# Attention of a two-layer diffusion block: exponentials turned by transposes, division at the values' eviction, outputs turned back per pair, and the next queries computed three units early

## The reference, cut to what matters

```
def attend(q, k, v):
    s = jnp.einsum('bqhd,bkhd->bhqk', q, k).astype(jnp.float32) * SOFTMAX_SCALE
    p = jax.nn.softmax(s, axis=-1).astype(v.dtype)
    return jnp.einsum('bhqk,bkhd->bqhd', p, v)
```

## Time and profile before

| | |
|---|---|
| median of three runs | 2633.77 us |
| profiled execution: its time, its span | 2636.96 us, 2635.1 us |
| busy: PE, DVE, ACT | 2461.8 us (93%), 1775.2 us (67%), 1396.1 us (53%) |
| chain that ended last | PE 86%, DVE 8%, ACT 3%, issue 1%, DMA 1% |
| attention, layer 0: first scores to first `gv` matmul | 160.03 to 291.56 us |
| attention, layer 1: the same | 1158.65 to 1234.29 us |

### The profile page before, as it was taken

How to read it: one execution, slowest core, us unless ns; L and a number is a source line. 1 busy time by engine, 2 the same in 40 slices (tenths; PEclk the granted TensorE clock), 3 DMA queues, 4 the chain that set the end, 5 groups by cost and what they waited for, 6 DMA issues and landing times.

```text
span 2635.1 us, 32564 instructions
## 1 busy us (share of the span) xinstructions
PE 2461.8 (93%) x12206; PEld 1980.5 (75%) x12206; DVE 1775.2 (67%) x1876; ACT 1396.1 (53%) x1495; POOL 42.5 (2%) x84
## 2 busy tenths in 40 slices
PE   6989999998999997878798599999999999999997
PEld 3756768884787885657697588888888888888886
DVE  3556863435333334667664788888989898989886
ACT  3354453334222222454554576777777777777775
POOL 0001000001000000000000000000000000000000
PEclk8988989999999998988898799999999999999998
DMA  7234223344434334211362798989999999999894
GB/s 270 78 120 136 80 64 104 112 162 167 143 110 130 117 94 145 80 64 47 96 202 75 287 371 341 377 341 356 361 353 354 354 370 343 371 356 362 340 374 183
DMA packets 104683, 579.23 MB, mean 220 GB/s; under 512 B 11920, under 2 KB 13840, under 8 KB 54800
## 3 DMA queue, kind: packets, MB, share of 16 engines
q1 hardware_dynamic: 93072, 536.04, 55.4%
q0 software_dynamic: 11520, 41.95, 4.7%
HBM read 576.89 MB, written 1.05 MB: 219 GB/s over the span
## 4 chain that ended last, share of the span: by engine, by line
PE 86%; DVE 8%; ACT 3%; issue 1%; DMA 1%; SPq 0%; DVEq 0%; ACTq 0%
PE bank L560 24%; PE bank L561 24%; PE bank L562 24%; PE bank L719 2%; PE bank L741 2%; PE bank L623 2%; PE bank L729 2%; DVE cacc L1453 1%; PE bank L913 1%; DVE rstd L1394 1%; PE bank L975 1%; PE bank L598 1%; DVE t L1409 1%; DVE al L1415 1%; DVE wlo L1374 1%
## 5 line engine op out<-in xcount | busy, mean ns | idle before, releaser
L1738 DVE TENSOR_TENSOR elo<-eraw,ehi 128x2048 fp32r<-128x2048 f32 x388 | 885.1, 2289 | 144.8 <-ACT ehi L1299 143.7
L1299 ACT CAST ehi<-eraw 128x2048 fp32r<-128x2048 f32 x388 | 742.4, 1916 | 263.1 <-PE bank L562 257.3
L1374 DVE TENSOR_TENSOR wlo<-raw,whi 128x1024 fp32r<-128x1024 f32 x220 | 269.5, 1225 | 298.6 <-ACT whi L1023 296.9
L560 PE MATMUL bank<-ah,whi 128*128 128x512 f32 (+1 forms) x1088 | 401.1, 369 | 23.4 <-DVE al L1415 15.6
L560 PE MATMUL bank<-ehi,xgh 128*128 128x512 f32 x1024 | 406.2, 397 | 17.9 <-DVE xgl L1744 17.9
L561 PE MATMUL bank<-elo,xgh 128*128 128x512 f32 x1024 | 400.1, 391 | 0.0
L562 PE MATMUL bank<-ehi,xgl 128*128 128x512 f32 x1024 | 399.6, 390 | 0.0
L561 PE MATMUL bank<-al,whi 128*128 128x512 f32 (+1 forms) x1088 | 392.1, 360 | 0.0
L562 PE MATMUL bank<-ah,wlo 128*128 128x512 f32 (+1 forms) x1088 | 391.9, 360 | 0.0
L1023 ACT CAST whi<-raw 128x1024 fp32r<-128x1024 f32 x220 | 229.6, 1044 | 119.1 <-PE bank L562 119.0
L560 PEld LDWEIGHTS bank<-ah,whi 128*128 128x128 f32 x1088 | 209.2, 192 | 70.6 <-DVE al L1415 17.5
(11 more groups left out here) (266 smaller groups left out, 2865.2 us busy)
## 6 DMA issues: line engine op xcount, KB each, us to landing
eraw<-in_moe SPq DMA_DIRECT2D x388, 1024.0 KB, 4.8
raw<-in_dense SPq DMA_DIRECT2D x220, 512.0 KB, 3.6
mod_b<-in_mod POOLq DMA_DIRECT2D x48, 512.0 KB, 4.9
mod_a<-in_mod POOLq DMA_DIRECT2D x32, 512.0 KB, 3.9
mod_s<-in_mod SPq DMA_DIRECT2D x16, 512.0 KB, 12.9
hres<-in_xT SPq DMA_DIRECT2D x1, 2048.0 KB, 8.3
wsT<-in_wsT SPq DMA_DIRECT2D x2, 512.0 KB, 8.5
out_h<-hres SPq DMA_DIRECT2D x2, 512.0 KB, 2.9
```

The source lines that it names most:

```text
L560: pe.matmul(dst, wh, xh, start=first, stop=False, skip_group_check=True)
L1299: nc.scalar.copy(ehi[c % ESPLIT][:], eraw[c % ERAW][:]).then_inc(e_hi, 1)
L1374: dve.tensor_tensor(wlo[c % SPLIT][:], raw[c % RAW][:], whi[c % SPLIT][:].bitcast(F32), ALU.subtract).then_inc(w_lo, 1)
L1738: dve.tensor_tensor(elo[c % ESPLIT][:], eraw[c % ERAW][:], ehi[c % ESPLIT][:].bitcast(F32), ALU.subtract).then_inc(e_lo, 1)
```

## The change

`turn` becomes plain transposes of the exponentials and waits for the exponential itself; `diag` and its ACT instruction go. `values` has the operands swapped: the turned exponentials are stationary (128x128), 64 columns of `V` move, and the output is 128 queries x 64 features. ACT divides when it evicts it, into a new tile `otok`. When all units of a pair are in `otok`, PE transposes it into an `acc_bank` (new step `outputs`), ACT copies that to `oh` and DVE subtracts for `ol`, one instruction each to a pair. Queries of pair j+1 are made in the step three before its first unit, into a second tile `qT2` that lies where `wsT` is; so `wsT` and `bsp` are loaded after the last scores, by SP, which waits for them. The end of the loop is one step later.

```
@@ plan: order of products
         for j in range(4):
             chunks.append(("uq", L, j))
             accs += [("uq", L, j, h) for h in range(2)]
+            if j > L:
+                accs.append(("ot", L, j - 1 - L))
+        accs += [("ot", L, j) for j in range(3 - L, 4)]
@@ tiles
-        rinv = place("rinv", [P, 2], F32)
+        rinv = place("rinv", [P, 4], F32)
-        diag = place("diag", [P, 2, P], F32, w1 + 36864)
+        qT2 = place("qT2", [QK_HEAD, 2, TOK], F32, wsT_at)
+        otok = place("otok", [P, 4, P], F32, std_at)
@@ new helpers
+        def pair_units(L):
+            return len(UNITS[L]) // 4
+        def query_pair(L, s):
+            j, r = divmod(s + 3, pair_units(L))
+            if s == 0:
+                return 0
+            return j if r == 0 and 1 <= j < 4 else None
+        def output_pair(L, s):
+            j, r = divmod(s - 3, pair_units(L))
+            return j - 1 if r == 0 and 1 <= j <= 4 else None
@@ SP
-                    if c == CHUNK[("q0", L)]:
-                        if L:
-                            sp.wait_ge(sp_done, 4 * L)
+                    if c == CHUNK[("gv", L, 2)]:
+                        sp.wait_ge(sc_ready, sum(len(UNITS[i]) for i in range(L + 1)))
                         sp.dma_start(wsT[:], A["wsT"][L]).then_inc(layer_landed, 16)
                         sp.dma_start(bsp[:], A["bsp"][L]).then_inc(layer_landed, 16)
@@ PE (queries(j): the 18 matmuls, moved out of scores unchanged)
                 def turn(u):
                     lo, hi = keys_of(units[u][2])
-                    pe.wait_ge(p_ready, base_u + u + 1)
+                    pe.wait_ge(exp_ready, base_u + u + 1)
                     if base_u + u:
                         pe.wait_ge(pt_ready, base_u + u)
                     for i in range((hi - lo) // P):
-                        mm = pe.matmul(TB[:, i * P:(i + 1) * P], pr[:, u % 2, i * P:(i + 1) * P], diag[:, u % 2, :],
-                                       start=True, stop=True, skip_group_check=True)
+                        mm = pe.transpose(TB[:, i * P:(i + 1) * P], pr[:, u % 2, i * P:(i + 1) * P], ident[:])
...
-                        mm = pe.matmul(o_bank[u % 2][64 * h:64 * h + 64, 0:P],
+                        mm = pe.matmul(o_bank[u % 2][:, 0:VH], pT[:, u % 2, i * P:(i + 1) * P],
                                        V[:, lo // P + i, (2 * j + h) * VH:(2 * j + h + 1) * VH],
-                                       pT[:, u % 2, i * P:(i + 1) * P], start=(i == 0), stop=(i == nk - 1))
+                                       start=(i == 0), stop=(i == nk - 1))
+                def outputs(j):
+                    pe.wait_ge(o_ready, base_u + (j + 1) * pair_units(L))
+                    b = bank(("ot", L, j))
+                    for t in range(nq // P):
+                        mm = pe.transpose(b[:, t * P:(t + 1) * P], otok[:, t, :], ident[:])
+                    mm.then_inc(ot_psum, 1)
...
-                for s in range(len(units) + 3):
+                for s in range(len(units) + 4):
+                    if s == 0:
+                        queries(0)
                     if s < len(units):
                         scores(s)
                     if 2 <= s <= len(units) + 1:
                         turn(s - 2)
-                    if s >= 3:
+                    if output_pair(L, s) is not None:
+                        outputs(output_pair(L, s))
+                    if 3 <= s <= len(units) + 2:
                         values(s - 3)
+                    if s and query_pair(L, s) is not None:
+                        queries(query_pair(L, s))
@@ ACT, step s: copies of the queries last; no diag; then
+                    out_j = output_pair(L, s)
+                    if out_j is not None:
+                        act.wait_ge(ot_psum, 4 * L + out_j + 1)
+                    if 3 <= s <= len(units) + 2:
                         u = s - 3
                         j, h, t = units[u]
+                        act.wait_ge(rinv_ready, base_u + u + 1)
                         act.wait_ge(o_psum, base_u + u + 1)
-                        nc.scalar.copy(oh[64 * h:64 * h + 64, j, t * P:(t + 1) * P],
-                                       o_bank[u % 2][64 * h:64 * h + 64, 0:P]).then_inc(x_hi, 1)
+                        nc.scalar.activation(otok[:, t, 64 * h:64 * h + 64], o_bank[u % 2][:, 0:VH], ACT.Copy,
+                                             scale=rinv[:, u % 4:u % 4 + 1]).then_inc(o_ready, 1)
+                    if out_j is not None:
+                        b = acc_bank[ACC[("ot", L, out_j)] % 2]
+                        nc.scalar.copy(oh[:, out_j, 0:nq], b[:, 0:nq]).then_inc(x_hi, 1)
+                    if s and query_pair(L, s) is not None:
+                        take_queries(query_pair(L, s))
@@ DVE, step s: row maximum and its negative first, then
+                    if 1 <= s <= len(units):
+                        u = s - 1
+                        dve.wait_ge(exp_ready, base_u + u + 1)
+                        if base_u + u >= 4:
+                            dve.wait_ge(o_ready, base_u + u - 3)
+                        dve.reciprocal(rinv[:, u % 4:u % 4 + 1], rsum[:, u % 2:u % 2 + 1]).then_inc(rinv_ready, 1)
+                    taps(TAPS_UNIT[L])
+                    out_j = output_pair(L, s)
+                    if out_j is not None:
                         dve.wait_ge(x_hi, n.next(x_hi))
+                        a = ACC[("ot", L, out_j)]
+                        dve.tensor_tensor(ol[:, out_j, 0:nq], acc_bank[a % 2][:, 0:nq],
+                                          oh[:, out_j, 0:nq].bitcast(F32), ALU.subtract).then_inc(acc_free[a % 2], 1)
+                    if s and query_pair(L, s) is not None:
+                        turn_queries(query_pair(L, s))
```

More of the change, by code:

```diff
@@ L393, in build @@
         o_ready = sem("o_ready")
+        ot_psum = sem("ot_psum")
         vt_ready = sem("vt_ready")
@@ L700, in _, with queries @@
                 units = UNITS[L]
+                def queries(j):
+                    wh, wl = weights(("uq", L, j))
+                    for hh_ in range(2):
+                        b = bank(("uq", L, j, hh_))
+                        for k in range(3):
+                            cols = slice((k * 2 + hh_) * P, (k * 2 + hh_ + 1) * P)
+                            mm = mm3(b[:, 0:nq], wh[:, cols], wl[:, cols], cnh[:, 2 + k, 0:nq],
+                                     cnl[:, 2 + k, 0:nq], k == 0, k == 2)
+                        mm.then_inc(chunk_used if hh_ else part, 1)
                 def scores(u):
@@ L704, in scores @@
                     if (h, t) == (0, 0):
-                        wh, wl = weights(("uq", L, j))
-                        for hh_ in range(2):
-                            b = bank(("uq", L, j, hh_))
-                            for k in range(3):
-                                cols = slice((k * 2 + hh_) * P, (k * 2 + hh_ + 1) * P)
-                                mm = mm3(b[:, 0:nq], wh[:, cols], wl[:, cols], cnh[:, 2 + k, 0:nq],
-                                         cnl[:, 2 + k, 0:nq], k == 0, k == 2)
-                            mm.then_inc(chunk_used if hh_ else part, 1)
                         taken(pe, ("uv", L, 3))
+                        taken(pe, ("uq", L, j, 0))
                         taken(pe, ("uq", L, j, 1))
@@ L1141, in _, with take_queries @@
                     act.wait_ge(const_landed, 16 * n_const)
-                for s in range(len(units) + 3):
-                    if L == 0 and s >= KD and s % KD == 0:
-                        copy_rows(1 + s // KD)
-                    if s < len(units):
-                        j, h, t = units[s]
-                        if (h, t) == (0, 0):
-                            for hh_ in range(2):
-                                key = ("uq", L, j, hh_)
-                                b, free = (await_acc if hh_ else await_part)(key, ("uq", L, j))
-                                if nq == TOK:
-                                    nc.scalar.copy(qT[64:96, hh_, LAT:TOK], b[64:96, LAT:TOK])
-                                nc.scalar.copy(qT[0:64, hh_, 0:nq], b[0:64, 0:nq]).then_inc(sig_ready, 1)
+                def take_queries(j):
+                    for hh_ in range(2):
+                        key = ("uq", L, j, hh_)
+                        b, free = (await_acc if hh_ else await_part)(key, ("uq", L, j))
+                        if nq == TOK:
+                            nc.scalar.copy(qT_of(j)[64:96, hh_, LAT:TOK], b[64:96, LAT:TOK])
+                        nc.scalar.copy(qT_of(j)[0:64, hh_, 0:nq], b[0:64, 0:nq]).then_inc(sig_ready, 1)
+                for s in range(len(units) + 4):
+                    if L == 0 and s >= KD and s % KD == 0 and s <= len(units):
+                        copy_rows(1 + s // KD)
+                    if s == 0:
+                        take_queries(0)
                     if 2 <= s <= len(units) + 1:
@@ L1161, in _ @@
```

(7 more changed lines are left out.)

51 lines of the change are left out of this document (18 added, 33 removed).

## The result

The changed kernel takes 2575.53 us (median of four runs, 2572.96 to 2579.59) against 2634.16 us for the kernel before on the same chip: ratio 0.9778, 95% interval 0.9758 to 0.9798. The prediction said 2579 us with a range of 2566 to 2603. Its profiled execution has a span of 2573.6 us where the one before had 2635.1, so 61.5 us have to be accounted for.

| stretch | before | after | difference |
|---|---|---|---|
| start to layer 0's first scores | 160.03 | 157.09 | -2.9 |
| layer 0, first scores to first `gv` matmul | 131.53 | 95.45 | -36.1 |
| from there to layer 1's first scores | 867.1 | 865.4 | -1.7 |
| layer 1, first scores to first `gv` matmul | 75.64 | 53.04 | -22.6 |
| from there to the end | 1400.8 | 1402.6 | +1.8 |

The account below looks back on a forecast made before the run. PE, 86% of the span, was taken as the bound, with DVE second. Layer 0's 38.5 us and layer 1's 16.8 sum to 55.3, taking 2633.8 to 2579 us, range 2566 to 2603 for 8 in 10.

Parts of the forecast that it names:

- Waits and clock, layer 0: Layer 0 attention: three query waits of 3.1 us go (9.4 us), and the low clock behind them (15.0 us).
- Turning: Layer 0 attention: four blocks turned in 0.44 us, two in 0.22, saving 13.9 us (range 13 to 16).
- Values: Layer 0 attention: the stationary side sets the pace, 0.94 us for eight records, 0.47 for four; saves 2.9 us.
- Added: Layer 0 attention: new transposes in `outputs` cost 1.8 us, and the loop's last step 0.5 us besides.
- A pair of layer 0: Layer 0 attention loop: a new pair takes 23.9 us, with PE still leading DVE.
- Transfers: Loads held behind the last scores cost nothing, at most 2 us; faster `mod_a` transfers cost nothing.
- Layer 1: Layer 1 attention: 56.2 us against 75.6, 19.4 saved, less 2.6 for one clock fall: 16.8 us.
- DVE's cycle: Layer 1 attention, from `outputs` 0 to `outputs` 1: DVE's work bounds the pair at 14.2 us.
- Gain kept behind layer 1: Layer 1's `gv` stage: the last taps end earlier by the same as attention, so its 19.4 us is kept.
- rival C: Behind layer 1's attention: the taps or a late `raw` hand its gain back; 2596 us, chance 4%.
- Rival A: Both attention loops: clock stays low; wholly low about 2705 us, slower than before 4%, mild form near 2600 us 12%.

Follow-up runs that it names:

- run with products: Changed kernel with turning by a plain fp32 product with the identity in place of transposes: 2587.13 us.
- wide values: Changed kernel with 128 moving columns of `V` instead of 64 in each product of values, the same 64 used: 2575.0 us.
- best kernel: Changed kernel with the first pair's queries made ahead of the values' products (`uv`) and `values(s-3)` issued ahead of `outputs`: 2567.33 us.
- values first: Changed kernel with `values(s-3)` issued ahead of the pair's `outputs` in a step: 2576.01 us.
- the split: Changed kernel with DVE doing the second head's rotary part, and the next weight chunk's split, one step later: 2585.98 us.

## Why the prediction was right

It came out 3.5 us above the measured median. The profiles differ by 61.5 us where it had 55.3, so the sum was 6.2 short; the median is nearer because the profiled execution of before lay some 3 us above its median. By its own steps:

- **Waits and clock, layer 0 (24.4 us).** Shown by the early queries alone: 23.4. The pairs' clock is 1.00 from the second on. The first pair's was 0.86, which I had not foreseen: the kernel before was at 1.00 there. The run with fewer taps, which has the same layer 0 code and held 1.00 throughout, needs 92.54 us where this needs 95.45, so the dip costs 2.9 us. It covers the whole difference between 38.5 us forecast and 36.1 found.
- **Turning (13.9 us).** 0.44 us for four blocks and 0.22 for two, as taken. The run with products puts 10.8 us of it down to the transposes themselves; the other 3 belong to the group behind the turning, whose stationary block is now 128x128.
- **Values (2.9 us).** 0.94 and 0.48, as taken (0.47); the row with the same stationary shape and 8 moving columns was the right neighbour.
- **Added (1.8 + 0.5 us).** `outputs` 0.43 each, and 0.47 of waiting before the last.
- **A pair of layer 0.** 23.84 us against 23.9.
- **Transfers.** `wsT` behind the scores delayed nothing: no wait of PE names them, and but for the 0.5 us before the last `outputs` the loop to `gv` is gapless.
- **Layer 1 (19.4 less 2.6 us).** It brought 22.6. Three terms were off. I took a fall of the clock behind one of the idle times (2.7 and 2.3 us forecast, 2.25 and 1.88 here), and none came in this profile: +2.6. That it did not is luck, as far as the runs show: in six variants with the same turning and early queries the clock fell inside this loop, and it took 57 to 63 us. PE's step was sized at 2.34 us with values at 0.94; values take 0.84 where scores follow them, as here, and the step is 2.2. DVE's step was sized at 2.33 us, with 1.45 for three taps from the earlier trace rows; it is 2.06, as here in the profile after:

```profile
1132.35 0.68 DVE L1592 TENSOR_REDUCE rowmax<-bank 128x1 f32<-128x512 f32 x1
1133.07 0.15 DVE L1593 TENSOR_SCALAR negmax<-rowmax 128x1 f32<-128x1 f32 x1
1133.15 0.16 DVE L1601 RECIPROCAL rinv<-rsum 128x1 f32<-128x1 f32 x1
1133.23 1.26 DVE L1492 SCALAR_TENSOR_TENSOR cacc<-up,par,cacc 128x256 f32<-128x256 f32 x3
1134.41 0.68 DVE L1592 TENSOR_REDUCE rowmax<-bank 128x1 f32<-128x512 f32 x1
```

  Three taps take 1.18 us. The trace of before had both: rows of 1.26 to 1.28 us for three taps in most steps of this loop and of 1.53 in its last ones, and I had read one of the last. The rows change when the first of two accumulators is done:

```profile
1223.20 0.40 DVE L1449 TENSOR_SCALAR cacc<-up,par 128x256 f32<-128x256 f32 x1
```

  Until then `taps` takes the two in turn, and afterwards each tap waits for the one just before it on the same accumulator, 0.48 us apart instead of 0.39. The chain came 14.4, 10.3, 13.2, 9.0 and 6.1 us where it said 14.8, 11.2, 14.2, 10.1 and 5.9. That PE is idle in front of the transposes of `otok`, behind a row maximum that stands behind the rotary parts, was right. That the cycle between two `outputs` is DVE's sum of work (14.2 us, "DVE's cycle") was not: it is the round trip of 13.24 us over PE, ACT and DVE, which stayed when four taps were taken out and grew by what PE's steps grew by with plain products. DVE's sum, near 12.6 us with the right price of the taps, lies close enough below it that the forecast hardly suffered.
- **Gain kept behind layer 1.** +1.8 us only, and the wait for the taps 7.43 against 7.29: rival C fell.
- **Outside the loops.** 2.8 us less in code that is the same, for which no term stood. So layer 0 fell short by 2.4 us, layer 1 gave 5.8 more and the rest 2.8: that they nearly cancel is in part luck.
- **Rival A's price.** 138 us wholly at the lower clock would give 2717 us, not the 2705 stated; no chance hung on it.

Rival A, the transposes that hold the clock down, was given 16% in both its forms. The loop of layer 0 ran at 1.00 with all its turning done by transposes (71 us of it in the changed kernel, 92.54 and 93.3 us in three variants), and plain products did not raise the clock where it was low. The rule of the Trainium skill (TensorE: Matmul & The Clock Gate, Part 4: PE-mode transpose), that transposes do not count for the higher clock as matmuls do, does not decide in a stage where they are mixed with other products; no run here tests a stage of transposes alone.

**What stays open** is when the clock falls in layer 1's loop. Its length follows the clock: 53.0, 53.1 and 54.6 us at 0.94 (changed kernel, wide values, best kernel), 57.0 to 60.7 at 0.82 and 0.83 (outputs later, values first, fewer taps, first queries early). But the idle times do not sort them. 2.25 and 1.88 us left it at 1.00 in the changed kernel, 1.88 was followed by a stretch at the lower level with fewer taps; 1.54 left it alone in the best kernel, and 1.55 with values first alone was followed by 0.67 over 5 us. Even one program differs from execution to execution: with the split, four runs took 2585.8 to 2586.3 us at a mean clock of 0.964 over the whole kernel, and one took 2578.38 at 0.967. So the 4.7 us by which the best kernel beats the one with the first queries early are a clock that stayed up, which no edit here can be said to have caused with certainty. Its 8.2 us over the changed kernel are not of that kind: its loop in layer 1 is 1.5 us longer than there.

## What to carry to other kernels

Where a matmul waits for a vector engine's work on its own operand, issue its producer some units early: the wait goes, and the stretches of low clock behind it may be worth more than the wait (some 14 of 23 us in layer 0 here). Fp32 blocks were turned by transposes at half the price of a product, and this paid although the scaling had to move to the next eviction for it. Before gains are added up on one engine, follow the next engine's sum through the loop and the stage behind it, and beside the sums the round trip through all engines: a busy engine need not be the bound, and taking work off it tells. Read a duration from the typical rows of a group, not from the last.

## What was not expected of the hardware

- A record with a 128x128 stationary fp32 operand costs 0.118 us with 64 moving columns, 0.122 with 128 (0.94 and 0.98 for eight), and 0.118 with 8. Part of it belongs to the group that follows: four records more cost 0.45 us (0.94 less 0.49, 0.98 less 0.54), 0.11 each, and the same eight values take 0.94 us ahead of the modulation and 0.84 ahead of scores. A plain fp32 product of a 128x128 block leaves two such records (0.89 us for four blocks), a transpose one (0.44).
- The same instructions before the same wait behave differently: with 3.22 us of idle time at the first scores of layer 0 the clock fell in the changed kernel and not in the ones with turning by products and with fewer taps. Up to that point all issue the same work on PE, and the last has the changed kernel's code through all of layer 0. From the profile after, then from the one with fewer taps:

```profile
157.09 1.10 PE L746 MATMUL bank<-kT,qT 96*128 96x512 f32 x2 [3.22 <-DVE qT L1581]
158.11 0.64 PE L647 MATMUL bank<-mod_a,cst 128*32 128x256 f32 x8
158.68 2.01 PE L746 MATMUL bank<-kT,qT 96*128 96x512 f32 x2
...
155.71 1.10 PE L746 MATMUL bank<-kT,qT 96*128 96x512 f32 x2 [3.22 <-DVE qT L1581]
156.74 0.64 PE L647 MATMUL bank<-mod_a,cst 128*32 128x256 f32 x8
157.31 1.13 PE L746 MATMUL bank<-kT,qT 96*128 96x512 f32 x2
```
